# A weight ring of twelve 1 MB slots against six 2 MB slots, in a decoder layer with 32 experts

## The reference: what is computed

```
def expert_block(args):
    xb, e = args
    h = xb @ w_gate_up[e] + b_gate_up[e]          # w_gate_up: [32, 1024, 2048]
    g, u = h[:, :D_EXPERT], h[:, D_EXPERT:]
    g = jnp.minimum(g, SWIGLU_LIMIT)
    u = jnp.clip(u, -SWIGLU_LIMIT, SWIGLU_LIMIT)
    glu = g * jax.nn.sigmoid(g * SWIGLU_ALPHA)
    return ((u + 1.0) * glu) @ w_down[e] + b_down[e]   # w_down: [32, 1024, 1024]
```

## Time and profile before

| | |
|---|---|
| median of 3 runs | 1299.18 us |
| lowest and highest | 1299.07, 1300.62 us |
| span of the profiled execution | 1298.2 us (no other time is listed for it) |
| TensorE busy | 1200.8 us, 93% |
| DVE, ACT, GpSimd busy | 247.6, 153.3, 56.9 us |
| DMA packets | 98,230, of them 65,408 under 8 KB; 445.33 MB |
| first gate/up matmul of expert 0 | 326.5 us |
| TensorE clock | 0.989 of 2.4 GHz in the mean |

### The profile page before, as it was taken

The page is one execution under the profiler, slowest core; times in us unless marked ns, Lnnn a source line. Parts: engine busy times, 40 slices in busy tenths (PEclk is TensorE's granted clock), DMA queues, the critical chain, the costliest instruction groups (busy, mean ns, idle before and its releaser), DMA issues.

```text
span 1298.2 us, 13406 instructions
## 1 busy us (share of the span) xinstructions
PE 1200.8 (93%) x5074; PEld 517.4 (40%) x5074; DVE 247.6 (19%) x587; ACT 153.3 (12%) x325; POOL 56.9 (4%) x60
## 2 busy tenths in 40 slices
PE   8999999996999999999999999999999999999995
PEld 6676745853333333333333333233333333333322
DVE  2122302115111111211111111112111111111114
ACT  2022221212010101010010101010100101010102
POOL 0011302112000000000000000000000000000000
PEclk9999999997999999999999999999999999999998
DMA  9941233354669999999999999999999999999993
GB/s 355 316 170 67 101 126 130 130 207 194 261 264 406 417 418 417 418 418 418 418 418 418 418 418 418 417 417 417 417 418 418 418 418 418 418 418 418 418 417 135
DMA packets 98230, 445.33 MB, mean 343 GB/s; under 512 B 13144, under 2 KB 14304, under 8 KB 65408
## 3 DMA queue, kind: packets, MB, share of 16 engines
q1 hardware_dynamic: 96192, 440.43, 84.4%
q10 hardware_dynamic: 2016, 4.60, 1.1%
HBM read 443.94 MB, written 1.06 MB: 343 GB/s over the span
## 4 chain that ended last, share of the span: by engine, by line
PE 57%; DMA 19%; SPq 15%; ACT 3%; issue 3%; DVE 2%; POOL 0%; DVEq 0%; ACTq 0%
DMA ring<-in_w_gate_up 19%; SPq L422 15%; PE bank L1357 14%; PE bank L1380 11%; PE bank L1066 9%; PE bank L1079 9%; PE bank L1284 5%; PE bank L1346 2%; PE bank L1333 2%; PE bank L1367 1%; ACT NCt L702 1%; ACT reg_k L675 1%; PE bank L1292 1%; PE bank L1231 1%; PE bank L1166 0%
## 5 line engine op out<-in xcount | busy, mean ns | idle before, releaser
L1357 PE MATMUL bank<-ring,PT 128*64 128x512 f32 x2008 | 445.1, 594 | 16.9 <-DMA ring<-in_w_gate_up 16.4
L1357 PEld LDWEIGHTS bank<-ring,PT 128*64 128x64 f32 x2008 | 140.3, 137 | 316.3 <-issue 254.5
L1380 PE MATMUL bank<-ring,NCt 128*64 128x512 f32 x1024 | 232.0, 600 | 23.5 <-ACT NCt L702 23.5
L1380 PEld LDWEIGHTS bank<-ring,NCt 128*64 128x64 f32 x1024 | 72.8, 137 | 150.8 <-issue 120.1
L976 DVE TENSOR_SCALAR reg_k<-bank 128x512 f32<-128x512 f32 x32 | 22.1, 692 | 481.6 <-PE bank L1357 481.6
L692 ACT ACTIVATE reg_v<-reg_k 128x512 f32<-128x512 f32 x32 | 20.1, 630 | 704.6 <-DVE reg_k L976 704.6
L1066 PE MATMUL bank<-reg_b,ring 128*128 128x256 f32 x384 | 84.6, 380 | 1.8 <-ACT reg_b L630 1.8
L994 DVE COPY vc<-bank 64x512 f32<-64x512 f32 x32 | 21.9, 684 | 314.1 <-PE bank L1380 314.1
L1066 PEld LDWEIGHTS bank<-reg_b,ring 128*128 128x128 f32 x384 | 72.5, 190 | 12.7 <-issue 3.1
L1284 PE MATMUL bank<-reg_a,L 128*128 128x512 f32 x136 | 64.8, 620 | 1.3 <-DVE L L919 1.3
L1333 PE MATMUL bank<-vc,L 128*128 128x512 f32 x128 | 59.2, 605 | 1.6 <-DVE vc L995 1.6
(11 more groups left out here) (198 smaller groups left out, 692.8 us busy)
## 6 DMA issues: line engine op xcount, KB each, us to landing
ring<-in_w_gate_up SPq DMA_DIRECT2D x251, 1024.0 KB, 20.2
ring<-in_w_down SPq DMA_DIRECT2D x128, 1024.0 KB, 22.4
ring<-in_w_in SPq DMA_DIRECT2D x6, 2048.0 KB, 15.4
ring<-in_w_ck SPq DMA_DIRECT2D x2, 2048.0 KB, 20.3
ring<-in_w_cv SPq DMA_DIRECT2D x2, 2048.0 KB, 10.1
ring<-in_w_mix_out SPq DMA_DIRECT2D x2, 2048.0 KB, 7.8
ring<-in_w_cq SPq DMA_DIRECT2D x2, 2048.0 KB, 7.9
ring<-in_w_co SPq DMA_DIRECT2D x2, 2048.0 KB, 9.6
```

The lines of the kernel that those rows point to most:

```text
L1357: last = mm(ps[half * CAP:(half + 1) * CAP, :], xgT[:, k, i * CAP:(i + 1) * CAP], w[:, c:c + HALF], start=False, stop=(k == KD - 1))
L1380: last = mm(xy_ps[half * CAP:(half + 1) * CAP, :], hT[:, a:a + CAP], w[:, j, half * HALF:(half + 1) * HALF], start=(k == 0), stop=(k == KD ...
```

## The change

The ring becomes six slots of 2 MB. A gate/up chunk is 256 rows of w_gate_up, and partition p holds the neighbouring rows 2p and 2p+1, 16 KB in one piece; a down chunk is 512 rows of w_down, and partition p holds the rows 4p to 4p+3, again 16 KB. The slot is waited for and freed once per chunk, after two k of gate/up or four k of down. Since a k then means every second or every fourth row, the transposes of Xg and hbuf take their columns with a step of 2 and of 4. Expert 1's first two chunks go into early buffers: chunk 0 into all of reg_q, and chunk 1 into reg_b and reg_c, which are now one buffer reg_bc, in two DMAs of 1 MB with 8 KB a partition each. The vectors of the second and third LayerNorm move to x_nat, and the output is built in reg_a. The first part's groups have one slot each, at the same places.

```
-CH = 12
-GUC = 8
+CH = 6
+GUC = 4
+GUJ = KD // GUC
+DNJ = KD // (CH - GUC)
+SLOT = GUJ * 2 * F
...
-        ring = sb("ring", [P, CH, 2048])
+        ring = sb("ring", [P, CH, SLOT])
...
-        reg_b = sb("reg_b", [P, KD, T])
-        reg_c = sb("reg_c", [P, KD, T])
+        reg_bc = sb("reg_bc", [P, 2, KD, T])
+        reg_b, reg_c = reg_bc[:, 0, :, :], reg_bc[:, 1, :, :]
...
-        lng = reg_q[:, 2048:3072]
-        lnb = reg_q[:, 3072:4096]
+        lng = [reg_q[:, 2048:3072], x_nat[:, 0, :], x_nat[:, 0, :]]
+        lnb = [reg_q[:, 3072:4096], x_nat[:, 1, :], x_nat[:, 1, :]]
...
+        y3 = mem_nat
...
-            return ring[:, 2 * s:2 * s + 2, :].rearrange("p a (b n) -> p (a b) n", n=HALF)
+            return ring[:, s, :].rearrange("p (k n) -> p k n", n=HALF)
...
-                w = w_gate_up[0][bass.ds(e, 1), c * P:(c + 1) * P, :]
-                return w.rearrange("o p n -> (o p) n")
-            w = w_down[0][bass.ds(e, 1), (c - GUC) * 2 * P:(c - GUC + 1) * 2 * P, :]
-            return w.rearrange("o (j p) n -> p (o j) n", p=P)
-
-        def in_slot(s, c):
-            return ring[:, s, :] if c < GUC else ring[:, s, :].rearrange("p (j n) -> p j n", j=2)
-
-
-        early = [x_nat[:, :, :].rearrange("p t d -> p (t d)"), reg_q[:, 0:2048], reg_c[:, :, :].rearrange("p k t -> p (k t)"),
-                 reg_q[:, 2048:4096], reg_b[:, :, :].rearrange("p k t -> p (k t)")]
+                w = w_gate_up[0][bass.ds(e, 1), c * GUJ * P:(c + 1) * GUJ * P, :]
+                return w.rearrange("o (p j) n -> p (o j) n", p=P)
+            w = w_down[0][bass.ds(e, 1), (c - GUC) * DNJ * P:(c - GUC + 1) * DNJ * P, :]
+            return w.rearrange("o (p j) n -> p (o j) n", p=P)
+
+        def rows_of(flat, c):
+            return flat.rearrange("p (j n) -> p j n", j=GUJ if c < GUC else DNJ)
+
+        early = [reg_q[:, :], reg_bc[:, :, :, :].rearrange("p a k t -> p (a k t)")]
...
-                return in_slot(c, c)
+                return rows_of(ring[:, c, :], c)
             if e == 1 and c < NEARLY:
-                return early[c]
-            return in_slot((c - NEARLY) % CH, c)
+                return rows_of(early[c], c)
+            return rows_of(ring[:, (c - NEARLY) % CH, :], c)
...
-            def load_early(c, left):
-
-                if c == 0:
-                    wait_evacuated(sp, left)
-                elif left:
-                    wait_filled(sp, left)
-                sp.wait_ge(chunk_in[c], 16)
-                sp.dma_start(early[c], chunk_source(1, c)).then_inc(chunk_in[c], 16)
...
-                    load_early(0, ("wo1", 1))
-                    load_early(2, ("cv1", 1))
-                    load_early(1, ("cqk", NCH - 1))
+
+                    wait_filled(sp, ("cv1", 1))
+                    sp.dma_start(chunk_tile(1, 1)[:, 1, :], chunk_source(1, 1)[:, 1, :]).then_inc(early_half_in, 16)
+                    wait_filled(sp, ("cqk", NCH - 1))
+                    sp.wait_ge(ln_out, TT)
+                    sp.wait_ge(chunk_in[0], 16)
+                    sp.dma_start(chunk_tile(0, 1), chunk_source(1, 0)).then_inc(chunk_in[0], 16)
                 wait_filled(sp, (GROUPS[n], 1))
-                for c in (2 * (n % GSLOTS), 2 * (n % GSLOTS) + 1):
-                    load_chunk(0, c, 0)
-            sp.wait_ge(ln_out, 2 * TT)
-            load_early(3, None)
-            load_early(4, ("rpart", 0))
+                load_chunk(0, n % GSLOTS, 0)
+
+            wait_filled(sp, ("rpart", 0))
+            sp.wait_ge(chunk_in[1], 16)
+            sp.dma_start(chunk_tile(1, 1)[:, 0, :], chunk_source(1, 1)[:, 0, :]).then_inc(chunk_in[1], 16)
...
-                    sp.dma_start(out[0, tt * P:(tt + 1) * P, cols], x_nat[:, tt, cols]).then_inc(stored, 16)
+                    sp.dma_start(out[0, tt * P:(tt + 1) * P, cols], y3[:, tt, cols]).then_inc(stored, 16)
...
-                act.dma_start(lng[:, :], g.to_broadcast([P, D])).then_inc(ln_in[i], 16)
-                act.dma_start(lnb[:, :], b.to_broadcast([P, D])).then_inc(ln_in[i], 16)
+                act.dma_start(lng[i], g.to_broadcast([P, D])).then_inc(ln_in[i], 16)
+                act.dma_start(lnb[i], b.to_broadcast([P, D])).then_inc(ln_in[i], 16)
...
                 pe.wait_ge((xg0_sb, xg1_sb)[half], m)
                 for j in range(4):
                     k = 4 * half + j
-                    last = nc.tensor.transpose((xy_ps, tr_ps)[half][:, j * P:(j + 1) * P], Xg[:, k * P:(k + 1) * P], ident)
+                    d = (k // GUJ) * GUJ * P + k % GUJ
+                    last = nc.tensor.transpose((xy_ps, tr_ps)[half][:, j * P:(j + 1) * P],
+                                               Xg[:, d:d + GUJ * (P - 1) + 1:GUJ], ident)
...
-                    pe.wait_ge(chunk_in[k], n * 16 + 16)
-                    w = chunk_tile(k, i if first else None)
+                    c, j = k // GUJ, k % GUJ
+                    if j == 0:
+                        pe.wait_ge(chunk_in[c], n * 16 + 16)
+                        if first and i == 1 and c == 1:
+                            pe.wait_ge(early_half_in, 16)
+                    w = chunk_tile(c, i if first else None)
                     for ps, c0 in ((gate_ps, 0), (up_ps, F)):
                         for half in range(2):
-                            c = c0 + half * HALF
+                            col = c0 + half * HALF
                             last = mm(ps[half * CAP:(half + 1) * CAP, :], xgT[:, k, i * CAP:(i + 1) * CAP],
-                                      w[:, c:c + HALF], start=False, stop=(k == KD - 1))
-                    if k < KD - 1:
+                                      w[:, j, col:col + HALF], start=False, stop=(k == KD - 1))
+                    if j == GUJ - 1 and k < KD - 1:
                         last.then_inc(chunks_used, 1)
...
-                    last = nc.tensor.transpose(tr_ps[:, j * P:(j + 1) * P], hbuf[:, j * P:(j + 1) * P], ident)
+                    last = nc.tensor.transpose(tr_ps[:, j * P:(j + 1) * P], hbuf[:, j:j + DNJ * (P - 1) + 1:DNJ], ident)
...
-                    c, j = GUC + k // 2, k % 2
+                    c, j = GUC + k // DNJ, k % DNJ
...
-                    if j and k < KD - 1:
+                    if j == DNJ - 1 and k < KD - 1:
```

More of the change, by code:

```diff
@@ L298, in hybrid_layer @@
         chunk_in = [sem(f"chunk_in{c}") for c in range(CH)]
+        early_half_in = sem("early_half_in")
         chunks_used = sem("chunks_used")
@@ L506, in gain_and_bias @@
                     wait_filled(pool, (tag, tt, 1))
-                    nc.gpsimd.tensor_tensor(dst[:, tt, :], dst[:, tt, :], lng, ALU.mult).then_inc(gained, 1)
+                    nc.gpsimd.tensor_tensor(dst[:, tt, :], dst[:, tt, :], lng[i], ALU.mult).then_inc(gained, 1)
                     pool.wait_ge(gained, TT * i + tt + 1)
-                    nc.gpsimd.tensor_tensor(dst[:, tt, :], dst[:, tt, :], lnb, ALU.add).then_inc(ln_out, 1)
+                    nc.gpsimd.tensor_tensor(dst[:, tt, :], dst[:, tt, :], lnb[i], ALU.add).then_inc(ln_out, 1)
             for h in range(NH):
@@ L524, in _ @@
                 pool.wait_ge(gained3, 2 * tt + 1)
-                nc.gpsimd.tensor_tensor(x_nat[:, tt, 0:HALF], x_nat[:, tt, 0:HALF], lnb[:, 0:HALF],
+                nc.gpsimd.tensor_tensor(y3[:, tt, 0:HALF], y3[:, tt, 0:HALF], lnb[2][:, 0:HALF],
                                         ALU.add).then_inc(biased_pool, 1)
@@ L721, in _ @@
                 for half in range(2):
-                    nc.scalar.activation(x_nat[:, tt, half * HALF:(half + 1) * HALF], acc[tt][half][:, :], ACT.Identity,
+                    nc.scalar.activation(y3[:, tt, half * HALF:(half + 1) * HALF], acc[tt][half][:, :], ACT.Identity,
                                          scale=rstd[:, 2, tt, 1:2], bias=mv[:, 2, tt, 1:2]).then_inc(normed, 1)
@@ L1021, in _ @@
                     dve.wait_ge(normed, 2 * tt + half + 1)
-                    nc.vector.tensor_tensor(x_nat[:, tt, cols], x_nat[:, tt, cols], lng[:, cols], ALU.mult).then_inc(gained3, 1)
+                    nc.vector.tensor_tensor(y3[:, tt, cols], y3[:, tt, cols], lng[2][:, cols], ALU.mult).then_inc(gained3, 1)
                 dve.wait_ge(gained3, 2 * tt + 2)
-                nc.vector.tensor_tensor(x_nat[:, tt, HALF:D], x_nat[:, tt, HALF:D], lnb[:, HALF:D],
+                nc.vector.tensor_tensor(y3[:, tt, HALF:D], y3[:, tt, HALF:D], lnb[2][:, HALF:D],
                                         ALU.add).then_inc(biased_dve, 1)
```

## The result

The changed kernel takes **1282.0 us** (1280.4 to 1283.2 in 4 runs) against 1299.2 for the kernel before in the same comparison: ratio 0.9863, 95% interval 0.9849 to 0.9877, so 17 us or 1.4% faster. The forecast was 1283.8.

A forecast was written before the change was run, and what follows sets the result against it. TensorE was taken to bound the kernel to about 670 us, the weight stream after it. -18.8 + 1.7 + 1.7 = -15.4 made the span 1282.8, the median 1283.8 us; range 1273 to 1296, own range 1279 to 1289.

The forecast's parts named there:

- What bounds: TensorE binds to about 670 us, the weight stream after it; a faster stream can give at most 25.7 us.
- Packets, -18.8: Weight stream: 16 KB packets cut 2.510 to 2.456 us a MB over 348 MB, 18.8 us less.
- 8.3 ns a packet: Price of one packet on each DMA engine, taken from windows of 8 KB and 4 KB packets.
- Rival 1: Weight stream: no gain past 8 KB packets, every MB costs 2.489 us; 1295.3 us in all, chance 0.13.
- Where the stream starts, +1.7: Expert 2's first down DMA waits for four of expert 1's down rows instead of two: 1.7 us later.
- Less preloaded, coarser slots later, 0: Buffers hold 16 MB instead of 17 before the experts, and later 2 MB slots come free later: both cost nothing.
- The end, +1.7: After the last gate/up chunk lands, TensorE works two rows instead of one before the gather: 1.7 us more.
- Transposes, 0: Loads of Xg with step 2 and hbuf with step 4 cost TensorE nothing; 57.68 us a pair stays.
- Rival 2: TensorE becomes the bound: step-4 transposes take twice as long, 0.88 us more a pair; 1286.7 us, chance 0.12.
- Rivals 3 and 4: 3: stepped loads cost four times, 1319.7 us, chance 0.10; 4: stream faster than TensorE, -25.7, 1273.5 us, chance 0.08.
- What would show it: Expected signs: 41,000 fewer packets, flat 427 GB/s, gathers 57.7 us apart to some 770 us, then 58.9.

The follow-up runs named there:

- experiment 7: The kernel before, with the DMAs of experts from the fourth on loading only 1 KB a partition, so TensorE runs without the stream: 1273.1 us.
- experiment 4: No run of its own: compares four kernels with different packet counts, at paces of 60.25, 59.66, 58.73 and 58.43 us a pair of experts.
- experiment 1: The changed kernel's six 2 MB slots, but with the old rows (packets of 8 and 4 KB) and transposes with a step of 1: 1303.4 us, ratio 1.0026.
- Experiment 9: The changed kernel with expert 2's two down chunks put into reg_q and reg_bc instead of ring slots: 1280.3 us, ratio 0.9849.

## Why the prediction was right

Forecast: -15.4; measured: -18.5 between the gathers, -17.2 in the medians. That the time missed by 1.8 us only, and the stretch by 3.1, is luck: the part ahead of the stretch came 1.4 later in the profiled execution, most of it for no reason that the change gives.

- **What bounds.** Right. TensorE's reserve was given as 25.7 us and is 25.8 (experiment 7).
- **Packets, -18.8.** The mechanism is right, the size was too small: 348 x (2.510 - 58.73 / 24) = 348 x 0.063 = -21.9. The step that failed is "8.3 ns a packet": I took it from the difference of two windows, 421 against 410 GB/s, where a whole GB/s is 0.006 us a MB and so 0.7 ns a packet. The printed figures allow 7.6 ns (421 against 411) to 8.7 (5.90 MB in 14 us against 4.10 in 10); 2.489 and 2.556 say more than those figures do. The paces of experiment 4 give 9.2 to 9.7. The view was right, its resolution was not. Rival 1 (no gain past 8 KB) falls, and so does its reading at 3.5 ns a packet: no step between 4 and 32 KB is under 9.2 ns. The 3.5 is the estimate from the 3 cycles a packet that the Trainium skill gives in "DMA: Bandwidth & Descriptors", "Why small descriptors are slow (HBM only)"; the measurement decides against it here.
- **Where the stream starts, +1.7.** 387.73 - 384.49 = 3.24, less the 1.44 by which the gathers lie later, is 1.8; experiment 1 shows 1.7. Experiment 9 takes the hole away.
- **Less preloaded, coarser slots later, 0.** Experiment 1 holds both and costs 3.3 us in all, no more than start and end together; its pace of 60.25 leaves nothing for slots that come free late.
- **The end, +1.7.** 3.65 us of gate/up between landing and gather, for 1.94.
- **Transposes, 0.** Wrong as a price, right in its effect. "No change, 57.68 a pair stays" became 57.95: two sets of hbuf at 0.10 more and one of Xg at 0.08 more (0.67 instead of 0.59). Over fifteen pairs that is 4.2 us on TensorE's own line, and the stream came 3.1 earlier than said: of the 10.3 us by which TensorE was to stay under the stream, 3.1 are left. Rival 2's mechanism is real at a third of its 0.88; from (872.37 - 865.10) / 15 = 0.48 a pair it would have decided. By the Trainium skill, "SBUF — State Buffer", the section on the DMA port swizzle, two accesses to a 16-byte line are wanted for full speed; fp32 has one with a step of 4 and two with a step of 2. The loads don't follow that: a step of 2 takes 209 ns in the median, a step of 4 213, a step of 1 141. The 1286.7 worked out for that case did not come.
- **Rivals 3 and 4.** No load costs four times, and the stream of 58.73 a pair is not under TensorE's 57.95, so 25.7 was not reached; but it came nearer to rival 4 than I thought.
- **What would show it.** 427 GB/s was said, 427 to 431 came; gathers 57.7 to 770 us and then 58.9 were said, 57.95 to 1015 and then 58.73 came: TensorE is slower and the stream faster than said, so they cross later. Of packets 41,000 fewer were said. 43,888 is 32 x 1280 for the rows, less 128 for reg_bc's 8 KB rows, and 3,056 packets under 512 B: 16 for each of 191 DMAs fewer.

## What to carry to other kernels

Where a weight stream binds, count packets an engine: what a merge of packets gives is their number times one price, here over 9 ns from 4 KB to 32 KB, and the price is best taken from the spacing of the waits over many rounds, not from GB/s in a short window. Then charge the ring for its slot size, once where the last hole ends and once behind the last landing; past the point where the two meet (here 16 KB) larger packets gave nothing. Before that, work out how much the next engine leaves to gain: here it was 25.8 us, and what an edit of the layout adds to that engine comes off it.

## What the runs showed that was not expected

- The price of a packet does not fall with its size: 9.2, 9.7 and 9.4 ns at 4 to 8, 8 to 16 and 16 to 32 KB. By that line a pair without any packets would take 58.73 - 96 x 0.0095 = 57.8 us (an estimate from these paces), about TensorE's pace.
- DMAs of 1 and of 2 MB in the same packets run at the same 60.25 us a pair, though the larger ones bring half as many of the packets under 512 B.
- A transposing weight load of 128x128 fp32 takes 141 ns with a step of 1, 209 with 2 and 213 with 4, and only 0.02 to 0.03 us of each reaches the chain.
